# Scale and shift of the first head's input made together, two slices at a time, with no corrections afterwards

## The chip, the core and the metric

One core of a Trainium2 chip runs the whole kernel. The metric is device time in microseconds (us) of one execution. Its engines work in parallel and meet at semaphores: PE multiplies matrices, DVE, ACT and POOL work on vectors, SP starts transfers.

## The reference

One layer of a two-branch backbone over 128 context and 512 latent tokens, 2048 channels wide, in fp32. The part that matters here is the input side:

```
mod   = silu(c) @ w_ada + b_ada             # c_ctx for context tokens, c for latent tokens
shift, scale, gate = split(mod, 3)          # 2048 values each
h     = rms_norm(x, norm_w) * (1 + scale) + shift
proj  = h @ w_in                            # 9 parts of 8 heads x 128 columns
rq, rk, rv, rg, hq, hf_f, hf_b, hi, hg = split(proj, 9)
```

Retention (rq, rk, rv, gate rg) and a gated recurrence (hq, forget gates hf_f and hf_b, hi, gate hg) follow for each head, in both directions; then one output projection, a gated residual and a norm.

## The kernel before

**Layout.** `h` is kept transposed: 16 slices of 128 channels, each 128 x 640 tokens. Every fp32 factor of the large products is split into a high and a low part (`hT_hi`, `hT_lo`, `w_hi`, `w_lo`), and a product is three matmuls, high*high, low*high and high*low. The weights of a head come as 18 chunks of 512 KB (`load`, L477) into three raw slots; `split` has ACT write the high part (L664) and DVE the low part (L1167) into two slots. The work of all engines is written out by hand, chunk by chunk (`items(n, h, prev)`, `stage(n, h, prev)`), and meets at semaphores; the order is that of the code.

**Heads 1 to 7** project in this order: chunks 0 and 1 the queries hq (`chunk`, 320 token columns per matmul, two halves), chunks 2 to 9 the group hf_f, hf_b, rq, rk (`group_chunk`: 512 latent columns at a time, and the context tokens with the weights as the moving side), chunks 10 to 17 the token parts (`token_chunk`, L2103 to L2105).

**Head 0** is another matter, since `h` isn't there yet when it starts. `w_ada` arrives as 32 pieces of 1 MB (`load_ada`, L445; four slots), and PE multiplies them with silu(c) (`ada_chunk`, L1895), 32 rows of the array for each quarter of the channels. DVE copies the sum to a row (`modulation_row`, L1175), PE turns it into columns (`modulation_columns`, L1903 to L1906) and DVE adds bias and norm weight (`modulation`, L1201, L1207). In the kernel before, the first 16 pieces give **scale** only, four slices at a time. With it the slices are scaled and split (L675 on ACT, L1226 on DVE; L1214 and L1232 for the first four), and PE projects three of the five column parts with them (`ahead`, L1920), then the other two (`chunk`, L2036). The other 16 pieces give **shift** and are multiplied between those projections (`between_slices`). Since the five column parts were projected without shift, their missing term shift @ w_in is computed from five more loads of 1 MB of plain weights (`w_first`, L447): `correction` (L1984), a copy on DVE (L1284), `correction_transposes` (L1991), and biases in the copies of ACT (`corrected`, L718 to L725). For the token parts the shift is added to the slices themselves, two slices per token chunk: DVE (`shifted_input`, L1271), ACT (L681) and POOL (L1813).

**Queue of transfers.** SP issues head 0's loads in a fixed order, each `w_ada` piece when PE has used the piece four before it.

Of the kernel before, what the change touches and what calls it, by code (L numbers as in the profile page):

```python
# [34 lines left out]
P = 128  # L35
D_MODEL = 2048
# [5 lines left out]
HEADS = 8  # L42
# [25 lines left out]
AHEAD = 3  # L68
UNITS = 2 * AHEAD
X_LOADS = 4  # L70
SQUARES = 4
CORRECTIONS = 5
# [45 lines left out]
def layer(nc, x_prompt, x_sample, s_ret_f, s_ret_b, s_hg_f, s_hg_b, c, c_ctx,  # L118
          w_out, final_norm_w, x_columns, vectors, w_mod, w_first, w_gate, gate_bias, w_in, consts,
          y_prompt, y_sample, n_ret_f, n_ret_b, n_hg_f, n_hg_b):  # L120
    ctx = ExitStack()
    with ctx:
# [23 lines left out]
        SMALL = 448 + P + 4 * TILES + 3 * KT  # L146
# [79 lines left out]
        shift = var[:, 0:KT * QUAD].rearrange("p (k m) -> p k m", k=KT)  # L226
        shifting = (newt, rstd)
        x_total_ps = ps.rearrange("p b n -> p (b n)")[:, 4 * 512:4 * 512 + T]
        corr_row = o_two
# [14 lines left out]
        corr = sc(2 * CORRECTIONS).rearrange("p (i w) -> p i w", w=2)  # L244
# [36 lines left out]
        h_mod, h_hi, h_lo = Signal("h_mod"), Signal("h_hi"), Signal("h_lo")  # L281
        s_mod, s_hi, s_lo = Signal("s_mod"), Signal("s_hi"), Signal("s_lo")
        corr_rows, corr_out, corr_ready = Signal("corr_rows"), Signal("corr_out"), Signal("corr_ready")
        z_exp, r_fixed = Signal("z_exp"), Signal("r_fixed")
# [55 lines left out]
        def proj(i):  # L340

            return ps[:, 2 * (i % 2):2 * (i % 2) + 2, 0:HALF]

        def first_head(h):
            return isinstance(h, int) and h == 0

        def ahead_banks(i):

            return (2, A, 0)[i]

        def part(h, i):

            if first_head(h) and i < AHEAD:
                return ps[:, ahead_banks(i):ahead_banks(i) + 2, 0:HALF]
            return proj(i)
# [43 lines left out]
        def new_queries(h):  # L399

            return o_one if first_head(h) else hq_next[:, :]

        def grouped(h, n):

            return not first_head(h) and QUERY_CHUNKS <= n < COLUMN_CHUNKS
# [11 lines left out]
        def mods_known(piece):  # L417

            return 2 * (piece + 1) if piece <= QUARTERS else piece + 2 + QUARTERS
# [8 lines left out]

        def shifted_slices(n):

            return range(4) if n == 9 else range(2 * n - 16, 2 * n - 14) if 10 <= n < 16 else range(0)
# [8 lines left out]
        def _(sp):  # L440
            def load_ada(c):
                if c >= ADA_SLOTS:
                    sp.wait_ge(a_used.sem, a_used.at(c - ADA_SLOTS))
                if c < ADA_CHUNKS:
                    sp.dma_start(ada_raw[:, c % ADA_SLOTS, :], w_mod[c]).then_inc(a_landed[c % ADA_SLOTS].sem, 16)  # L445
                else:
                    sp.dma_start(ada_raw[:, c % ADA_SLOTS, :], w_first[c - ADA_CHUNKS]).then_inc(a_landed[c % ADA_SLOTS].sem, 16)  # L447
# [2057 lines left out]
```

## Time and profile before

| | us |
|---|---|
| median of 3 runs | 1438.04 (1437.69 to 1439.27) |
| the profiled execution | 1438.13 |
| its span in the trace | 1436.2 |
| PE busy | 1414.6 (98%) |
| DVE busy | 980.4 (68%) |
| ACT busy | 508.2 (35%) |
| POOL busy | 394.1 (27%) |

The profiled execution is 0.09 us above the median, and 1.9 us of it lie outside the span. In a window row, each engine's busy us stand with its instruction count in brackets, then PE's granted clock as a share of full speed, the mean busy share of the 16 transfer engines, and what they moved. In a timeline row, the first number is the start, the second the busy time of the merged instructions; a bracket gives idle time before and who ended it. PE matmuls overlap, so the pitch is the distance of starts. A plain fp32 matmul shows as two.

### The profile page before, as it was taken

The numbers are of one execution on the slowest core, as the hardware profiler recorded it, in microseconds if no ns is written. First come the engines' busy times: TensorE is split into PE (matmuls) and PEld (weight loads), VectorE is DVE, ScalarE is ACT, GpSimd is POOL, SyncE is SP. The second block draws the span as 40 slices with busy tenths as digits, with TensorE's granted clock in tenths as the row PEclk, the third lists the DMA queues.
The fourth block names the chain that finished last, engine by engine and source line by source line (L and its number), as shares of the span: only waits on it lengthen the run. The fifth ranks groups of instructions, "written<-read, shape, count | busy, mean of one in ns | idle before, by whom it ended". The sixth has DMA issues, their size and how long they took to land.

```text
span 1436.2 us, 26292 instructions
## 1 busy us (share of the span) xinstructions
PE 1414.6 (98%) x10558; PEld 1204.3 (84%) x10558; DVE 980.4 (68%) x1306; ACT 508.2 (35%) x912; POOL 394.1 (27%) x308
## 2 busy tenths in 40 slices
PE   7999999999999999999999999999999999999997
PEld 6998798889888988898889888988898888788886
DVE  5733996666878687878887888666566748632345
ACT  4322543333332433343334333433342334221234
POOL 0001563411342144214321532153115315301220
PEclk9999999999999999999999999999999999999999
DMA  9998322324333334333333333222223347183235
GB/s 379 378 363 356 92 90 74 96 67 141 114 134 94 127 126 126 101 125 124 119 99 121 126 118 110 67 81 89 96 67 96 87 149 255 46 279 117 88 103 205
DMA packets 69303, 201.93 MB, mean 141 GB/s; under 512 B 7872, under 2 KB 16336, under 8 KB 63440
## 3 DMA queue, kind: packets, MB, share of 16 engines
q1 hardware_dynamic: 69168, 200.39, 40.5%
q8 instruction: 83, 1.36, 0.4%
q14 instruction: 20, 0.16, 0.0%
q10 hardware_dynamic: 32, 0.02, 0.0%
HBM read 179.65 MB, written 16.53 MB: 137 GB/s over the span
## 4 chain that ended last, share of the span: by engine, by line
PE 93%; DMA 2%; DVE 2%; POOL 1%; ACT 1%; issue 1%; SPq 0%; DVEq 0%; ACTq 0%
PE ps L2103 10%; PE ps L2105 9%; PE ps L2104 9%; PE ps L2036 9%; PE ps L2056 7%; PE ps L2058 7%; PE ps L2057 7%; PE ps L2285 5%; PE ps L2287 5%; PE ps L2286 5%; PE ps L1920 3%; PE ps L2122 2%; PE ps L1895 2%; PE ps L2067 2%; PE ps L2065 2%; PE ps L2066 2%
## 5 line engine op out<-in xcount | busy, mean ns | idle before, releaser
L1167 DVE TENSOR_TENSOR w_lo<-area,w_hi 128x1024 fp32r<-128x1024 f32 x144 | 193.5, 1344 | 259.5 <-ACT w_hi L664 259.0
L664 ACT ACTIVATE w_hi<-area 128x1024 fp32r<-128x1024 f32 x144 | 152.4, 1058 | 469.4 <-PE ps L2105 243.9
L2103 PE MATMUL ps<-w_hi,hT_hi 128*128 128x512 f32 x640 | 253.5, 396 | 2.8 <-DVE w_lo L1167 2.8
L2105 PE MATMUL ps<-w_hi,hT_lo 128*128 128x512 f32 x640 | 249.6, 390 | 0.0
L2104 PE MATMUL ps<-w_lo,hT_hi 128*128 128x512 f32 x640 | 249.3, 390 | 0.0
L2056 PE MATMUL ps<-hT_hi,w_hi 128*128 128x512 f32 x448 | 178.0, 397 | 0.0
L2057 PE MATMUL ps<-hT_lo,w_hi 128*128 128x512 f32 x448 | 174.5, 390 | 0.0
L2058 PE MATMUL ps<-hT_hi,w_lo 128*128 128x512 f32 x448 | 174.5, 390 | 0.0
L2103 PEld LDWEIGHTS ps<-w_hi,hT_hi 128*128 128x128 f32 x640 | 120.2, 188 | 29.6 <-DVE w_lo L1167 3.9
L1790 POOL TENSOR_TENSOR area<-area 128x320 f32<-128x320 f32 x56 | 53.9, 963 | 326.3 <-PE ps L2122 273.7
L2105 PEld LDWEIGHTS ps<-w_hi,hT_lo 128*128 128x128 f32 x640 | 120.1, 188 | 25.4
L2104 PEld LDWEIGHTS ps<-w_lo,hT_hi 128*128 128x128 f32 x640 | 120.3, 188 | 23.6
L2285 PE MATMUL ps<-w_hi,hT_hi 128*128 128x512 f32 x296 | 116.9, 395 | 0.9 <-DVE w_lo L1632 0.9
L2287 PE MATMUL ps<-w_hi,hT_lo 128*128 128x512 f32 x296 | 115.4, 390 | 0.0
L2286 PE MATMUL ps<-w_lo,hT_hi 128*128 128x512 f32 x296 | 115.3, 390 | 0.0
L1632 DVE TENSOR_TENSOR w_lo<-area,w_hi 128x1024 fp32r<-128x1024 f32 x32 | 43.4, 1355 | 94.9 <-ACT w_hi L1010 94.8
L2058 PEld LDWEIGHTS ps<-hT_hi,w_lo 128*128 128x128 f32 x448 | 84.1, 188 | 17.8
L2056 PEld LDWEIGHTS ps<-hT_hi,w_hi 128*128 128x128 f32 x448 | 84.1, 188 | 17.5
L2057 PEld LDWEIGHTS ps<-hT_lo,w_hi 128*128 128x128 f32 x448 | 84.2, 188 | 16.4
L839 ACT ACTIVATE area<-area 128x1280 f32<-128x1280 f32 x56 | 71.2, 1275 | 70.9 <-DVE area L1435 66.3
L1421 DVE SCALAR_TENSOR_TENSOR gate_sums<-gate_raw,small,gate_sums 128x512 f32<-128x512 f32 x128 | 90.5, 767 | 0.0
L1801 POOL TENSOR_TENSOR area<-area 128x320 f32<-128x320 f32 x56 | 62.3, 1113 | 85.4 <-ACT area L839 85.4
(300 smaller groups left out, 2650.5 us busy)
## 6 DMA issues: line engine op xcount, KB each, us to landing
area<-in_w_in SPq DMA_DIRECT2D x144, 512.0 KB, 3.7
area<-in_w_mod SPq DMA_DIRECT2D x32, 1024.0 KB, 9.2
area<-in_w_out SPq DMA_DIRECT2D x38, 512.0 KB, 3.7
gate_raw<-in_w_gate SPq DMA_DIRECT2D x32, 512.0 KB, 3.7
area<-in_x_columns SPq DMA_DIRECT2D x4, 1280.0 KB, 9.7
area<-in_w_first SPq DMA_DIRECT2D x5, 1024.0 KB, 8.1
o_hi_scratch<-area SPq DMA_DIRECT2D x14, 320.0 KB, 2.2
o_lo_scratch<-area SPq DMA_DIRECT2D x14, 320.0 KB, 2.8
```

The costliest lines, as they stand in the source:

```text
L664: act.activation(w_hi[:, n % 2, :], raw[:, n % 3, :], ACT.Copy).then_inc(wt_hi.sem, 1)
L1167: v.tensor_tensor(w_lo[:, n % 2, :], raw[:, n % 3, :], w_hi[:, n % 2, :].bitcast(F32), ALU.subtract).then_inc(wt_lo.sem, 1)
L2036: ins = mm(out[s], wt[:, n % 2, w], x[:, k, s * HALF:(s + 1) * HALF], start=k == 0 and step == 0, stop=k == KT - 1 and step == 2)
L2056: mm(ps[:, bank, :], w_hi[:, n % 2, w], hT_hi[:, k, P:T], start=k == 0, stop=False)
L2057: mm(ps[:, bank, :], w_hi[:, n % 2, w], hT_lo[:, k, P:T], start=False, stop=False)
L2058: ins = mm(ps[:, bank, :], w_lo[:, n % 2, w], hT_hi[:, k, P:T], start=False, stop=k == KT - 1)
L2103: mm(out, hT_hi[:, k, tile_cols(t)], w_hi[:, n % 2, w], start=k == 0, stop=False)
L2104: mm(out, hT_hi[:, k, tile_cols(t)], w_lo[:, n % 2, w], start=False, stop=False)
L2105: i = mm(out, hT_lo[:, k, tile_cols(t)], w_hi[:, n % 2, w], start=False, stop=k == KT - 1)
L2285: mm(out, hT_hi[:, k, tile_cols(t)], hi, start=k == first, stop=False)
L2286: mm(out, hT_hi[:, k, tile_cols(t)], lo, start=False, stop=False)
L2287: return mm(out, hT_lo[:, k, tile_cols(t)], hi, start=False, stop=k == final)
```

## The change

Scale and shift come together. Piece order of `w_ada` is changed: a run of four pieces holds scale and shift of **two** slices (the first slice and the second slice have two pieces each). DVE normalizes a pair of slices ahead (`normed_input`), then multiplies and adds in one instruction (`modulated_input`), and the high and low parts hold the finished `h`. Head 0 then projects the same group as the other heads, slice by slice, all four parts (`first_group`), from chunks in the group's layout; the queries follow as chunks 8 and 9, in banks C and DD; the token parts need no shift any more. `correction`, `shifted_input`, `corrected`, `first_gates` and the five loads `w_first` are gone, and head 0 uses the group's copies, context transposes and reciprocals.

```diff
-            chunks = {6: 1, 9: 2, 11: 3, 13: 4, 15: 5, 17: 6, 20: 7, 24: 8, 28: 9, 32: 10, 36: 11}
-            for c_ in range(ADA_CHUNKS + CORRECTIONS):
+            chunks = {6: 1, 10: 2, 14: 3, 18: 4, 22: 5, 26: 6, 30: 7}
+            for c_ in range(ADA_CHUNKS):
                 load_ada(c_)
                 if c_ in chunks:
                     load(0, chunks[c_])
+            load(0, 8)
...
+            for e in range(WCHUNKS):                    # ACT
+                for k in range(WK * e, WK * (e + 1)):
+                    high_input(k)
+                if e < WCHUNKS - 1:
+                    split(0, e + 1)
...
+            def modulated_input(k):                     # DVE
+                dve.wait_ge(h_norm.sem, h_norm.at(k))
+                for w, tokens in CLASSES:
+                    x = x_in[:, k, tokens]
+                    i = v.tensor_scalar(x, x, mods[:, w, k:k + 1], shifts[:, w, k:k + 1], ALU.mult, ALU.add)
+                i.then_inc(h_mod.sem, 1)
...
+            for e in range(1, WCHUNKS):
+                split(0, e)
+                for k in range(WK * e, WK * (e + 1)):
+                    normed_input(k)
+                modulation_row(e + 1)
+                modulation(e + 1)
+                for k in range(WK * e, WK * (e + 1)):
+                    modulated_input(k)
+                for k in range(WK * e, WK * (e + 1)):
+                    low_input(k)
...
+            for e in range(1, WCHUNKS - 1):             # PE
+                c0 = (e + 1) * GROUP_CHUNKS
+                first_group(e, 0)
+                for c_ in range(c0, c0 + GROUP_CHUNKS):
+                    ada_chunk(c_)
+                first_group(e, 1, range(0, 1))
+                modulation_columns(e + 2)
+                first_group(e, 1, range(1, 5))
+            first_group(WCHUNKS - 1, 0)
+            first_group(WCHUNKS - 1, 1)
...
-            def correction(m):
-                for k in range(KT):
-                    rows = slice(k % 4 * QUAD, (k % 4 + 1) * QUAD)
-                    ins = mm(out[rows, :], shift[:, k, :], ada_raw[:, slot, tile_cols(k)], start=k < 4, stop=k >= KT - 4)
```

How PE's order moves, in the middle of the stage that makes the slices. Before (L1895 multiplies pieces of `w_ada`, 16 matmuls for one; L1920 are projections of one part; L1906 turns the row into columns):

```order
L1920 MATMUL ps<-hT_lo,w_hi 128x320 x2
L1920 MATMUL ps<-hT_hi,w_lo 128x320 x2
L1895 MATMUL ps<-area 32x128 x64
L1920 MATMUL ps<-hT_hi,w_hi 128x320 x2
L1920 MATMUL ps<-hT_lo,w_hi 128x320 x2
L1920 MATMUL ps<-hT_hi,w_lo 128x320 x2
L1906 MATMUL ps<-con,area 128x128
L1920 MATMUL ps<-hT_hi,w_hi 128x320 x2
```

After (L1744 to L1746 a part of the group, L1751 to L1753 the context tokens, L1728 the pieces, L1739 the columns):

```order
L1751 MATMUL ps<-w_hi,hT_hi 128x512
L1752 MATMUL ps<-w_lo,hT_hi 128x512
L1753 MATMUL ps<-w_hi,hT_lo 128x512
L1728 MATMUL ps<-area 32x128 x64
L1744 MATMUL ps<-hT_hi,w_hi 128x512
L1745 MATMUL ps<-hT_lo,w_hi 128x512
L1746 MATMUL ps<-hT_hi,w_lo 128x512
L1739 MATMUL ps<-con,area 128x128
L1744 MATMUL ps<-hT_hi,w_hi 128x512
```

A run of four pieces stood between projections worth 12 slice-parts of four slices before; after, between the 15 matmuls of the pair's first slice and the 15 of its second.

How DVE's order moves for the same stage. Before, one run of four slices (L1175 row, L1201 and L1207 columns, L1226 low parts, L1167 weights, L1220 and L1221 the normalizing of a later slice):

```order
L1175 COPY area<-ps 128x128
L1201 TENSOR_TENSOR small<-ps,small 128x4 x2
L1207 SCALAR_TENSOR_TENSOR small<-small 128x4 x2
L1226 SCALAR_TENSOR_TENSOR hT_lo<-area,small,hT_hi 128x128
L1226 SCALAR_TENSOR_TENSOR hT_lo<-area,small,hT_hi 128x512
...
L1167 TENSOR_TENSOR w_lo<-area,w_hi 128x1024
L1220 TENSOR_TENSOR area<-area 128x128
L1221 TENSOR_TENSOR area<-area 128x512
```

After, one pair (L1093 row, L1116 to L1119 scale and shift columns, L1132 multiply and add, L1137 low parts, L1085 the next weights):

```order
L1093 COPY area<-ps 128x128
L1116 TENSOR_TENSOR small<-ps,small 128x2x2
L1117 TENSOR_TENSOR small<-ps,small 128x2x2
L1119 SCALAR_TENSOR_TENSOR small<-small 128x2x2
L1132 TENSOR_SCALAR area<-area,small 128x128
L1132 TENSOR_SCALAR area<-area,small 128x512
L1132 TENSOR_SCALAR area<-area,small 128x128
L1132 TENSOR_SCALAR area<-area,small 128x512
L1137 TENSOR_TENSOR hT_lo<-area,hT_hi 128x640 x2
L1085 TENSOR_TENSOR w_lo<-area,w_hi 128x1024
```

Between the columns and the first low part stand four multiply-and-adds on DVE, and ACT's high part; before, ACT scaled and split in one instruction beside DVE.

At the end of the stage, on PE before, the last corrections stand ahead of the first token chunk:

```order
L2036 MATMUL ps<-hT_hi,w_lo 128x320 x2
L1984 MATMUL ps<-area 32x128 x48
L2103 MATMUL ps<-w_hi,hT_hi 128x512
L2104 MATMUL ps<-w_lo,hT_hi 128x512
L2105 MATMUL ps<-w_hi,hT_lo 128x512
```

After, the queries (L1839) stand right ahead of the first token chunk (L1889 to L1891):

```order
L1839 MATMUL ps<-hT_lo,w_hi 128x320 x2
L1839 MATMUL ps<-hT_hi,w_lo 128x320 x2
L1889 MATMUL ps<-w_hi,hT_hi 128x512
L1890 MATMUL ps<-w_lo,hT_hi 128x512
L1891 MATMUL ps<-w_hi,hT_lo 128x512
```

The five corrections and their transposes (L1991, inside the first token chunk) have gone, and nothing stands in their place there.

## Rows read from the trace of the kernel before

**Rows 1.** The page: the span, and each engine's busy us, share and instructions.

```profile
span 1436.2 us, 26292 instructions
PE 1414.6 (98%) x10558; PEld 1204.3 (84%) x10558; DVE 980.4 (68%) x1306; ACT 508.2 (35%) x912; POOL 394.1 (27%) x308
```

**Rows 2.** PE's waits: total us, times, longest us.

```profile
PE ps L2103 <- DVE w_lo L1167: 2.8, 2, 1.5
```

**Rows 3.** Windows of 10 us (columns as told above).

```profile
0.00:10.00 10.00, 5.21 (x26) 4.97 (x27) 1.61 (x8) 3.62 (x6) 0.20 (x4) 1.00 0.74 274
...
60.00:70.00 10.00, 10.00 (x172) 9.60 (x172) 6.40 (x14) 1.55 (x2) 0.00 (x0) 1.00 0.87 340
...
100.00:110.00 10.00, 10.00 (x171) 9.40 (x164) 4.83 (x22) 1.94 (x6) 0.00 (x0) 1.00 1.02 424
...
120.00:130.00 10.00, 10.00 (x144) 9.21 (x143) 2.70 (x7) 1.06 (x1) 0.00 (x0) 1.00 1.01 415
...
170.00:180.00 10.00, 8.74 (x39) 6.93 (x38) 9.61 (x12) 6.29 (x12) 6.34 (x3) 1.00 0.32 98
```

**Rows 4.** Loads from 0 to 142 us: count, size, median us from issue to landing.

```profile
area<-in_w_mod SPq DMA_DIRECT2D x32, 1024.0 KB, 9.2
area<-in_w_in SPq DMA_DIRECT2D x14, 512.0 KB, 8.7
area<-in_x_columns SPq DMA_DIRECT2D x4, 1280.0 KB, 9.7
```

**Rows 5.** PE's timeline: fillers, pieces of w_ada, projections of 320 columns.

```profile
27.65 2.50 PE L1929 MATMUL ps<-con 128*128 128x128 f32 x20
...
50.70 3.70 PE L1895 MATMUL ps<-area 128*32 128x128 f32 x128
54.33 0.56 PE L1920 MATMUL ps<-hT_hi,w_hi 128*128 128x320 f32 x2
...
55.71 0.45 PE L1920 MATMUL ps<-hT_lo,w_hi 128*128 128x320 f32 x2
56.00 0.46 PE L1920 MATMUL ps<-hT_hi,w_lo 128*128 128x320 f32 x2
...
65.19 3.70 PE L1895 MATMUL ps<-area 128*32 128x128 f32 x128
```

**Rows 6.** PE's timeline around and in the first token chunks.

```profile
136.66 1.08 PE L1984 MATMUL ps<-area 128*32 128x128 f32 x32 [0.68 <-DMA area<-in_w_first]
137.68 0.50 PE L2103 MATMUL ps<-w_hi,hT_hi 128*128 128x512 f32 x1
...
140.54 1.20 PE L1991 MATMUL ps<-con,area 128*128 128x32 f32 x10
141.58 0.48 PE L2103 MATMUL ps<-w_hi,hT_hi 128*128 128x512 f32 x1
...
150.51 0.39 PE L2103 MATMUL ps<-w_hi,hT_hi 128*128 128x512 f32 x1
...
158.44 0.39 PE L2105 MATMUL ps<-w_hi,hT_lo 128*128 128x512 f32 x1
```

**Rows 7.** Groups of DVE and ACT, 0 to 142 us: busy us, mean ns, idle before.

```profile
L1167 DVE TENSOR_TENSOR w_lo<-area,w_hi 128x1024 fp32r<-128x1024 f32 x12 | 14.7, 1223 | 15.8 <-ACT w_hi L664 15.6
L1221 DVE TENSOR_TENSOR area<-area 128x512 f32<-128x512 f32 x12 | 8.2, 684 | 0.0
L1232 DVE TENSOR_TENSOR hT_lo<-area,hT_hi 128x640 fp32r<-128x640 f32 x4 | 3.3, 822 | 0.1
L669 ACT ACTIVATE hT_hi<-area 128x640 fp32r<-128x640 f32 x4 | 2.9, 737 | 10.2 <-DVE area L1214 10.2
L1175 DVE COPY area<-ps 128x128 f32<-128x128 f32 x9 | 2.6, 291 | 24.3 <-PE ps L1895 20.3 <-issue 4.0
```

**Rows 8.** Groups over the whole span, for instructions the change adds to head 0.

```profile
L1550 DVE TENSOR_SCALAR area<-area,small 128x640 f32<-128x640 f32 x14 | 7.9, 607 | 0.0
L2075 PE MATMUL ps<-con,area 128*128 128x128 f32 x28 | 4.2, 272 | 0.0
```

More of the change, by code:

```diff
@@ L1906, in modulation_columns, with group_part @@
                     nc.tensor.transpose(ps[:, ada_bank(piece), 0:P], mod_row, ident).then_inc(row_tr.sem, 1)
-            def ahead(s, kks=range(ADA_K)):
-                n, quarter, i = s // 2, s // AHEAD, s % AHEAD
-                if kks[0] == 0 and s % 2 == 0:
-                    pe.wait_ge(wt_lo.sem, wt_lo.at(0, n + 1))
-                for kk in kks:
-                    k = quarter * ADA_K + kk
-                    w = slice((s % 2) * ADA_K * P + kk * P, (s % 2) * ADA_K * P + (kk + 1) * P)
-                    if i == 0:
-                        pe.wait_ge(h_lo.sem, h_lo.at(k))
-                    for step, (wt, x) in enumerate(((w_hi, hT_hi), (w_hi, hT_lo), (w_lo, hT_hi))):
-                        for half in range(2):
-                            ins = mm(ps[:, ahead_banks(i) + half, 0:HALF], wt[:, n % 2, w], x[:, k, half * HALF:(half + 1) * HALF],
-                                     start=k == 0 and step == 0, stop=k == KT - 1 and step == 2)
-                if kks[-1] == ADA_K - 1 and s % 2:
-                    ins.then_inc(wt_used.sem, 1)
+            def group_part(n, kk, i, k):
+                bank, w = GROUP_BANKS[i], slice(kk * WIDE + i * P, kk * WIDE + (i + 1) * P)
+                mm(ps[:, bank, :], w_hi[:, n % 2, w], hT_hi[:, k, P:T], start=k == 0, stop=False)
+                mm(ps[:, bank, :], w_hi[:, n % 2, w], hT_lo[:, k, P:T], start=False, stop=False)
+                return mm(ps[:, bank, :], w_lo[:, n % 2, w], hT_hi[:, k, P:T], start=False, stop=k == KT - 1)
@@ new lines, in group_context, with first_group @@
+            def group_context(n, kk, k):
+                w = slice(kk * WIDE, (kk + 1) * WIDE)
+                mm(ps[:, BB, :], hT_hi[:, k, 0:P], w_hi[:, n % 2, w], start=k == 0, stop=False)
+                mm(ps[:, BB, :], hT_hi[:, k, 0:P], w_lo[:, n % 2, w], start=False, stop=False)
+                return mm(ps[:, BB, :], hT_lo[:, k, 0:P], w_hi[:, n % 2, w], start=False, stop=k == KT - 1)
+            def first_group(e, kk, places=range(len(GROUP_PARTS) + 1)):
+                k = WK * e + kk
+                if kk == 0 and places[0] == 0:
+                    pe.wait_ge(wt_lo.sem, wt_lo.at(0, e + 1))
+                if places[0] == 0:
+                    pe.wait_ge(h_lo.sem, h_lo.at(k))
+                for i in places:
+                    if i < len(GROUP_PARTS):
+                        ins = group_part(e, kk, i, k)
+                        if k == KT - 1:
+                            ins.then_inc(pe_group.sem, 1)
+                    else:
+                        ins = group_context(e, kk, k)
+                        if kk == WK - 1:
+                            ins.then_inc(wt_used.sem, 1)
@@ L2048, in group_chunk @@
                 pe.wait_ge(wt_lo.sem, wt_lo.at(h, n + 1))
-                for i, bank in enumerate(GROUP_BANKS):
+                for i in range(len(GROUP_PARTS)):
                     if j == 0 and i == 0:
```

440 lines of the change are left out of this document (106 added, 334 removed).

## The prediction

> **What bounds the kernel now.** I read the page first. PE is busy 1414.6 of 1436.2 us, every other engine has slack [rows 1]. So time comes only from fewer or denser matmuls, or from PE's idle 21.6 us. The list of waits says where that is: behind the start-up, the largest is 2.8 us in two stalls of head 0's token chunks, waiting for the low weights of DVE [rows 2]. I then read the windows of head 0, the only head that the change rewrites. From 100 to 130 us PE is full and the transfers are full as well, 415 to 424 GB/s at a share above 1.0; from 60 to 70 us they reach 340, because SP must wait for slots that PE frees [rows 3]. So this stage has two limits close together, and the change moves both. From 140 us on transfers are idle and DVE is the busy one: 9.61 of 10 us between 170 and 180, where PE drops to 8.74 [rows 3]. Last I read PE's timeline: the first token chunk starts at 137.68 us, right behind the last correction, which had waited 0.68 us for its load [rows 6]. That instant is the mark against which I build the new stage.
>
> **Durations.** A 320-column matmul has a pitch of 0.147 us (two in 0.29) [rows 5]. A 512-column one has 0.2266 (35 from 150.51 to 158.44) [rows 6]. One slice through four parts is 24 of the first, 3.52 us, before, and 15 of the second, 3.40 us, after. Over 16 slices the change of form saves 1.9 us; the queries stay in the old form, 96 x 0.147 = 14.1. A run of four pieces of `w_ada` takes 3.63 (50.70 to 54.33). From run to run are 14.49 us, of which 72 matmuls take 10.56, so switching kinds and turning the row into columns cost 0.30 a run [rows 5].
>
> **PE through the new stage, step by step.** The fillers end at 30.15 [rows 5]. Piece 3 now stands ahead of them: 31.1. Two slices of the first pair (6.8), four pieces (3.8), 0.3 for columns and form changes, 0.3 for small waits: the second pair's run ends at 42.3.
>
> Then the first new wait. For pair 1 nothing lies between the run and the first slice that needs it. The chain is: row copy 0.29, columns, three small DVE operations, multiply-and-add, ACT's high part 0.74, low part 0.82 [rows 7]. The multiply-and-add is not in the trace in two pieces; as one over 640 columns with two per-partition scalars it takes 0.61 [rows 8], and that is my value. It can't be below it, and at worst is as slow as a two-tensor pass, 0.68 on 512 columns and some 0.2 for the short piece, 0.9 [rows 7]. The three small ones have no row of their form; each lies between nothing and the 0.29 of the row copy, and I take 0.5 for all with their waits (ends 0 and 0.9). Sum: 0.36 + 0.3 + 0.5 + 0.6 + 0.8 + 0.9, about 3.6. PE idles until 45.9; slice 3.4, run 3.8: the next run ends at 53.1.
>
> For pairs 2 to 6 the second slice of the pair before (3.40, plus 0.30) covers the chain. With the transposes placed behind the first part the chain is 0.3 longer, 3.95: PE stalls 0.25. PE's cycle is 3.63 + 6.80 + 0.30 + 0.25 = 11.0. The transfers' cycle is 4 x 1024 KB + 512 KB = 4.72 MB [rows 4], at 419 GB/s (mean of the two full windows) 11.25. Both are so near that the waits of the one at times add to the other: I take 11.3, five times 56.5, and 0.6 more for the first, since during the 3.6 us stall the four slots are full and SP can't issue. So the last run ends at 110.2. Transfers alone give a floor: by then 43.25 MB have to come (5.24 of x, 4.19 of weights, 33.55 of `w_ada`, 0.26 small), 2.74 in the first 10 us [rows 3], the rest at 419 GB/s: 106.7, and 0.95 for the last piece. Behind the run: the second slice with columns 3.7, stall 0.25, two slices 6.8: 120.95. Queries 14.1 and 0.1 for the switch: the token chunks start at **135.1, 2.6 us earlier**. The five corrections (L1984) with their wait and five loads of 1 MB are inside these 2.6 us, since 137.68 counted them.
>
> ACT evacuates the group and splits chunk 9 beside the queries, 7 us ahead of need. Chunk 8 is queued behind the last `w_ada` piece and lands some 10 us ahead of its use. The two con loads moved behind it are used only from the rotary step on. If one of these covers failed, PE would wait at the queries for 1.05 + 1.22, 2.3 us.
>
> **Token stage.** The five transposes of the corrections stand in the first token chunk: 140.54 to 141.58, 1.04 us gone [rows 6]. The two stalls of 2.8 us go [rows 2]: DVE loses 32 shift additions; it gains two context operations, a reciprocal, and four affine operations of 0.5 to 0.6 that ACT did, about 6 us against some 15 to 20. The new dependence is the context transposes, four fp32 ones on PE: 4 x 0.11 if pipelined, 4 x 0.27 if not [rows 8]; I take 0.45. They wait for ACT's context copy, made a whole query stage earlier. The retention scores wait for the rotated rk; its inputs are there at about 121 us, some 50 us ahead.
>
> **Sum.** 2.6 + 1.04 + 2.8 - 0.45 = 6.0 us less than the profiled execution's own 1438.13 (span 1436.2 [rows 1] and 1.9 outside it): 1432.1. That execution is 0.09 us above the median of the runs, so I forecast **1432.0 us**. Ends of the unknown prices: 0.3 to 0.6 more per pair for multiply-and-add and small operations, 5 pairs and the first, 3.6 us; the stalls half gone instead of gone, 1.4; the transposes 0.6; against it 0.25 x 5 + 1.5 if the two limits overlap perfectly. The forecast's own range is 1429.0 to 1435.1.
>
> **A rule against the change.** At 100 to 130 us the load stream reads 415 to 424 GB/s with DVE, ACT and PE at work [rows 3]. The Trainium skill (DMA: Bandwidth & Descriptors, Bandwidth, Where 436 GB/s comes from) says that for HBM-to-SBUF transfers the HBM side, about 358 GB/s per core, binds; its own table has 425 for one core on large transfers. By the 358 the 40.5 MB would take an estimated 113 us instead of 96.7, and this change would be a loss, some 1448. The trace disagrees with the 358, so I give that only a small chance.
>
> The granted clock stays 1.00 in the first 10 us, in which PE is busy for only 5.21 [rows 3]. The Trainium skill (TensorE: Matmul & The Clock Gate, What's actually happening) has idleness halve the clock. If the 3.6 us wait of pair 1 did so, the next slice would run at the lower level, 3.4 us more; the row at the start speaks against it.
>
> **Rivals.**
> *PE paces the stage.* Transfers run ahead, the chain fits under the slice. For it: 11.0 against 11.25 is thin, and the low parts of the first slice come early. Then five cycles at 10.8 and no 0.6: 3.1 us less, 1428.9. Against it: the floor of 106.7 lies only 3.5 us below my 110.2, so not much more can come.
>
> *The saving is eaten, no change to speak of.* The chain is a microsecond longer per pair (DVE's weight split and the normalizing, 1.22 + 1.6 us [rows 7], stand ahead of the row copy, and the weights of a pair land only one piece before its last). Each microsecond by which that group is late is paid by PE. Landing 3.5 us before the run's end, it is late by 0.4; at 1 us late, less 0.25 of slack to the transfers, 5 x 0.75 = 3.8: 1435.8. Against it: a slower PE lets the transfers get ahead, so the lateness limits itself.
>
> *Slower: the stage is bound by transfers below 419 GB/s.* Before, 4 MB came for 12 slice-parts of work in these cycles, 14.49 us [rows 5]; now for 8, so each per cent of rate costs 1 us of stage. The place is the wait of `ada_chunk` for its piece. From 10 us on 40.5 MB have to come, 96.7 us at 419 GB/s; it decides when that is 8.9 us longer (my 1432.0 to 1440.9, 0.2% above before), at 384 GB/s. At 340, the rate of the window 60 to 70 [rows 3], it would be 22.4 us longer: 1454.4. For it: that window. Against it: there the slots were empty by PE's order, and with the queue full no window is under 415.
>
> *The change doesn't do what it says*: corrections remain in some form. Excluded by the order on PE.
>
> **Chances.** Forecast 0.52, PE-paced 0.12, eaten 0.24, slower by transfers or by a chain too long 0.12. Measurement of this kernel can tell about 0.2%, 2.9 us, from no change: faster is under 1435.2, slower over 1440.9. The first two cases are faster, 0.64; the third is the same, 0.24; the last slower, 0.12. The range that should hold eight times in ten is 1428.5 to 1438.5.
>
> **What the profile after would show.** Right: waits of PE for low slices (hT_lo), one of about 3 us near 43 us and small ones after; waits for w_mod of 0 to 1 us per run; pitch 0.227 in the group; runs 11.3 us apart; transfers above 415 GB/s from 55 to 107 us; the first token chunk at about 135; no wait of head 0 for w_lo. Wrong: runs 12 us apart or more (then see whether hT_lo or w_mod ends the wait), a wait at the queries, the w_lo stalls still there, or a granted clock below 1.00 near 46 us.

## The result: slower by 0.3%, where 0.4% faster was forecast

| | before | after | forecast of after |
|---|---|---|---|
| median us (range, runs) | 1437.96 (1437.69 to 1439.27, 7) | 1442.84 (1441.77 to 1444.63, 7) | 1432.0 |
| profiled execution, us | 1438.13 | 1444.63 | 1432.1 |
| first token chunk of head 0 | 137.68 | 148.57 | 135.1 |
| first matmul of head 1 | 198.50 | 205.07 | 192.5 |

The ratio after to before is 1.0031, with a 95% interval of 1.0021 to 1.0041. The profiled execution of after is the slowest of its seven; the places below are read from it, so up to 1.8 us of its time are its own. The time lies outside the range of the forecast (1428.5 to 1438.5), in the case "slower", which had 0.12.

The loss is all ahead of head 1: its first matmul is 6.57 us late, the span 6.8 us longer. Inside head 0 the two halves have opposite signs. From the first token chunk to head 1, before took 60.8 us and after 56.5: 4.3 less, with 3.4 forecast. The stage that makes the slices ends 10.9 us later than before, where 2.6 earlier was forecast: the whole miss, 13.5 us, is there.

### The profile page after: what moved, and what is told of

Read it like the earlier page. It is cut to its first block, busy times and chain, and to the rows that moved or that the text cites. A ratio compares the mean times of both kernels' runs of the same rounds, so it can differ in the third digit from the quotient of the medians.

```text
span 1443.0 us, 25582 instructions
## 1 busy us (share of the span) xinstructions
PE 1412.7 (98%) x10247; PEld 1191.0 (83%) x10247; DVE 959.5 (66%) x1292; ACT 488.8 (34%) x877; POOL 360.2 (25%) x292
## 4 chain that ended last, share of the span: by engine, by line
PE 92%; DMA 5%; DVE 1%; SPq 1%; ACT 0%; issue 0%; POOL 0%; DVEq 0%; ACTq 0%
PE ps L1889 10%; PE ps L1891 10%; PE ps L1890 10%; PE ps L1744 8%; PE ps L1839 8%; PE ps L1746 8%; PE ps L1745 8%; DMA area<-in_w_mod 5%; PE ps L2069 5%; PE ps L2071 5%; PE ps L2070 5%; PE ps L1906 2%; PE ps L1753 2%; PE ps L1751 2%; PE ps L1752 2%; PE ps L1728 1%
## 5 line engine op out<-in xcount | busy, mean ns | idle before, releaser
L1085 DVE TENSOR_TENSOR w_lo<-area,w_hi 128x1024 fp32r<-128x1024 f32 x144 | 187.4, 1302 | 312.1 <-ACT w_hi L642 311.5
L1889 PE MATMUL ps<-w_hi,hT_hi 128*128 128x512 f32 x640 | 253.2, 396 | 0.0
L1891 PE MATMUL ps<-w_hi,hT_lo 128*128 128x512 f32 x640 | 249.5, 390 | 0.0
L1744 PE MATMUL ps<-hT_hi,w_hi 128*128 128x512 f32 x512 | 206.5, 403 | 4.8 <-DVE hT_lo L1137 4.8
L1746 PE MATMUL ps<-hT_hi,w_lo 128*128 128x512 f32 x512 | 200.9, 392 | 0.0
L1745 PE MATMUL ps<-hT_lo,w_hi 128*128 128x512 f32 x512 | 200.6, 392 | 0.0
L1889 PEld LDWEIGHTS ps<-w_hi,hT_hi 128*128 128x128 f32 x640 | 120.2, 188 | 25.6 <-issue 1.6
L1891 PEld LDWEIGHTS ps<-w_hi,hT_lo 128*128 128x128 f32 x640 | 120.1, 188 | 25.5
L1744 PEld LDWEIGHTS ps<-hT_hi,w_hi 128*128 128x128 f32 x512 | 97.0, 189 | 28.2 <-issue 8.5
L1746 PEld LDWEIGHTS ps<-hT_hi,w_lo 128*128 128x128 f32 x512 | 96.7, 189 | 21.0
L1745 PEld LDWEIGHTS ps<-hT_lo,w_hi 128*128 128x128 f32 x512 | 97.1, 190 | 18.5
L1472 DVE TENSOR_TENSOR w_lo<-area,w_hi 128x1024 fp32r<-128x1024 f32 x32 | 43.4, 1357 | 96.3 <-ACT w_hi L928 96.2
```

The lines of the kernel that those rows point to most:

```text
L1085: v.tensor_tensor(w_lo[:, n % 2, :], raw[:, n % 3, :], w_hi[:, n % 2, :].bitcast(F32), ALU.subtract).then_inc(wt_lo.sem, 1)
L1744: mm(ps[:, bank, :], w_hi[:, n % 2, w], hT_hi[:, k, P:T], start=k == 0, stop=False)
L1745: mm(ps[:, bank, :], w_hi[:, n % 2, w], hT_lo[:, k, P:T], start=False, stop=False)
L1746: return mm(ps[:, bank, :], w_lo[:, n % 2, w], hT_hi[:, k, P:T], start=False, stop=k == KT - 1)
L1889: mm(out, hT_hi[:, k, tile_cols(t)], w_hi[:, n % 2, w], start=k == 0, stop=False)
L1891: i = mm(out, hT_lo[:, k, tile_cols(t)], w_hi[:, n % 2, w], start=False, stop=k == KT - 1)
```

## The profile after

The page: PE is busy for 1.9 us less than before [rows 1], the span is 6.8 longer; PE waits more.

```profile
span 1443.0 us, 25582 instructions
PE 1412.7 (98%) x10247; PEld 1191.0 (83%) x10247; DVE 959.5 (66%) x1292; ACT 488.8 (34%) x877; POOL 360.2 (25%) x292
```

PE's waits. The stall of [rows 2] is gone; pieces of w_ada (L1728), low slices (L1744) and the row (L1739) hold it up now.

```profile
PE ps L1728 <- DMA area<-in_w_mod: 7.4, 5, 2.1
PE ps L1744 <- DVE hT_lo L1137: 4.8, 6, 3.1
PE ps L1739 <- DVE area L1093: 0.4, 1, 0.4
```

Windows, to lay beside [rows 3]. The granted clock is no longer 1.00 throughout, and the transfers have holes in the stage that was forecast as bound by them.

```profile
30.00:40.00 10.00, 10.00 (x111) 8.68 (x115) 3.06 (x9) 1.69 (x2) 0.00 (x0) 0.83 0.92 378
...
50.00:60.00 10.00, 9.75 (x148) 8.04 (x149) 3.96 (x8) 1.06 (x1) 0.00 (x0) 0.83 0.60 228
60.00:70.00 10.00, 9.34 (x125) 7.36 (x123) 3.62 (x10) 2.51 (x3) 0.00 (x0) 1.00 1.01 419
...
80.00:90.00 10.00, 9.56 (x153) 7.78 (x153) 6.51 (x15) 2.51 (x3) 0.00 (x0) 1.00 0.88 342
...
100.00:110.00 10.00, 9.54 (x154) 7.48 (x153) 4.89 (x11) 2.03 (x3) 0.00 (x0) 1.00 0.88 338
...
120.00:130.00 10.00, 8.53 (x59) 6.82 (x60) 7.45 (x16) 2.62 (x4) 0.00 (x0) 0.83 0.54 215
```

PE's timeline answers to [rows 5] and shows the start and pair 1. Piece 3, ahead of the fillers (L1776) by the change, is waited for 2.04 us. Then it takes 1.76 us where the same 32 matmuls took 1.08 three us earlier, and the fillers 3.42 where before they took 2.50. The first slice starts at 34.86. At pair 1, behind its wait of 3.08 us, two matmuls stand at the pitch of 0.3, and then seven at 0.43: 1.2 GHz instead of 2.4.

```profile
26.87 1.08 PE L1728 MATMUL ps<-area 128*32 128x128 f32 x32
...
30.00 1.76 PE L1728 MATMUL ps<-area 128*32 128x128 f32 x32 [2.04 <-DMA area<-in_w_mod]
31.68 3.42 PE L1776 MATMUL ps<-con 128*128 128x128 f32 x20
34.86 0.48 PE L1744 MATMUL ps<-hT_hi,w_hi 128*128 128x512 f32 x1
...
46.85 0.33 PE L1739 MATMUL ps<-con,area 128*128 128x128 f32 x1 [0.41 <-DVE area L1093]
50.25 0.47 PE L1744 MATMUL ps<-hT_hi,w_hi 128*128 128x512 f32 x1 [3.08 <-DVE hT_lo L1137]
50.56 0.48 PE L1745 MATMUL ps<-hT_lo,w_hi 128*128 128x512 f32 x1
50.84 0.63 PE L1746 MATMUL ps<-hT_hi,w_lo 128*128 128x512 f32 x1
51.26 0.63 PE L1744 MATMUL ps<-hT_hi,w_hi 128*128 128x512 f32 x1
...
53.82 0.54 PE L1744 MATMUL ps<-hT_hi,w_hi 128*128 128x512 f32 x1
54.20 0.39 PE L1745 MATMUL ps<-hT_lo,w_hi 128*128 128x512 f32 x1
...
55.45 3.70 PE L1728 MATMUL ps<-area 128*32 128x128 f32 x128
```

The chain of waits from 59 to 98 us (start, us, what) names what sets the later pairs. It closes on itself: a load of w_ada is issued when PE has used the fourth piece of a run; it lands 10.5 to 11.9 us later; it is itself the fourth piece of the next run; PE multiplies it, 1.1 us; the next load is issued. (From 97 to 109 us the chain runs over PE's slices instead; then it is back on a load, 12.1 us.)

```profile
59.87 11.34 DMA area<-in_w_mod
...
71.25 1.12 PE ps L1728 x32
...
72.39 10.51 DMA area<-in_w_mod
...
82.95 1.06 PE ps L1728 x29
...
84.09 11.89 DMA area<-in_w_mod
...
96.02 1.08 PE ps L1728 x32
```

And the hole at 80 us: SP issues nothing between 72.8 and 81.15, since all four slots are taken and PE multiplies slices. The transfers' share sinks with it.

```profile
81.15 2.08 SPq L425 DMA_DIRECT2D area<-in_w_mod  x3
```

```profile
56.00:80.00 24.00, 21.77 (x306) 17.33 (x298) 10.82 (x26) 3.96 (x5) 0.00 (x0) 1.00 0.94 380
80.00:84.00 4.00, 3.89 (x130) 3.42 (x129) 2.45 (x5) 1.06 (x1) 0.00 (x0) 1.00 0.70 231
```

So I had three suspects. **A, slots:** one run uses as many pieces as there are slots, so PE's use and the refill add up instead of overlapping. **B, chain:** the modulation on DVE and ACT (3.08 + 0.41 us at pair 1, 0.33 to 0.35 at five more) sets the cycle. **C, clock:** what costs is the low clock behind the waits.

## The experiments

Each was run beside the kernel before on the same chip. An interval reaches 1.2 to 2.3 us to each side, so two gains that differ by less than some 2 us can't be told apart by the medians. "Tokens" is the start of the first token chunk in the profiled execution (137.68 before, 148.57 after, 135.1 forecast).

| kernel | median us | before beside it | ratio, 95% interval | tokens |
|---|---|---|---|---|
| fifth slot | 1436.78 | 1438.55 | 0.9988 (0.9979 to 0.9997) | 140.87 |
| two and two | 1434.96 | 1438.55 | 0.9973 (0.9963 to 0.9984) | 139.64 |
| start in the old order | 1441.47 | 1438.55 | 1.0019 (1.0010 to 1.0029) | 145.80 |
| half loads | 1434.34 | 1438.55 | 0.9971 (0.9959 to 0.9983) | 139.13 |
| fillers in pair 1's wait | 1440.90 | 1438.97 | 1.0010 (1.0001 to 1.0018) | 145.34 |
| start + two and two | 1432.67 | 1438.97 | 0.9951 (0.9939 to 0.9964) | 137.69 |
| the same + fifth slot | 1432.68 | 1438.97 | 0.9952 (0.9939 to 0.9965) | 136.08 |
| start + fifth slot | 1435.40 | 1438.97 | 0.9972 (0.9962 to 0.9982) | 138.57 |
| kernel before + fifth slot | 1438.22 | 1439.24 | 0.9993 (0.9984 to 1.0002) | 136.88 |
| weights last | 1455.60 | 1439.24 | 1.0108 (1.0093 to 1.0124) | 160.12 |
| fillers first | 1440.78 | 1439.24 | 1.0009 (1.0000 to 1.0018) | 144.17 |
| three things mended | 1432.99 | 1439.15 | 0.9955 (0.9941 to 0.9968) | 137.75 |

### A fifth slot

```diff
-ADA_SLOTS = 4
+ADA_SLOTS = 5
+        def ada_slot(slot):
+            return ada_four[:, slot, :] if slot < 4 else gate_raw.rearrange("p s n -> p (s n)")
```

> One edit to the changed kernel: a fifth 1 MB slot for the pieces of w_ada, in space that is free until the gate's weights come. Theory A (slots and landing: a run uses four pieces in 3.6 us out of four slots, so the transfers stand still 2.3 to 2.5 us in every second cycle, and the last piece is released some 2 us behind its bytes): PE's waits for w_mod after the first pair (5.2 us in three pieces) go to under 1 us, runs 11.3 us apart instead of 12.7, and the time falls by 4 to 6 us, to 1437 to 1439. Theory B (chain: the modulation chain of DVE and ACT sets the pair's cycle): no change beyond 0.5 us, the waits for hT_lo grow by what those for w_mod lose. Theory C (clock: the lower granted clock behind each wait is what costs): at most 1 us, by the one low stretch behind run 7.

Against before it stands 6.6 us better than the changed kernel did (1.8 below it instead of 4.9 above). A had expected 4 to 6, so the gain is a little larger. Its window from 60 to 110 us: 413 GB/s, no hole. Its timeline around 80 us: a run without a wait for its fourth piece, and then 0.35 us for the low slice; six such waits stand 11.4 us apart.

```profile
60.00:110.00 50.00, 48.24 (x655) 38.95 (x654) 29.75 (x69) 11.49 (x14) 0.00 (x0) 1.00 1.01 413
```

```profile
77.94 2.83 PE L1732 MATMUL ps<-area 128*32 128x128 f32 x96
80.58 1.06 PE L1732 MATMUL ps<-gate_raw,area 128*32 128x128 f32 x32
81.57 0.50 PE L1748 MATMUL ps<-hT_hi,w_hi 128*128 128x512 f32 x1
...
85.73 0.47 PE L1748 MATMUL ps<-hT_hi,w_hi 128*128 128x512 f32 x1 [0.35 <-DVE hT_lo L1141]
```

The waits for hT_lo did not grow: the chain was not hidden behind the loads. A holds, B and C alone fall. Of the 7.7 us at the tokens, 6.5 lie in the five cycles and 0.9 behind them, where the changed kernel's profile has a low stretch and this one has none. With a slot more than a run uses the cycle is 11.4, near the forecast's 11.3; but PE no longer waits for a piece in it, so it is PE's own cycle, 11.05 and the 0.35 of waiting for the low slice, where the forecast had 10.7 and 0.25.

### Two pieces behind each slice

```diff
                 first_group(e, 0)
-                for c_ in range(c0, c0 + GROUP_CHUNKS):
-                    ada_chunk(c_)
+                ada_chunk(c0 + 2)
+                ada_chunk(c0 + 3)
                 first_group(e, 1, range(0, 1))
                 modulation_columns(e + 2)
                 first_group(e, 1, range(1, 5))
+                if e < WCHUNKS - 2:
+                    ada_chunk(c0 + 4)
+                    ada_chunk(c0 + 5)
```

> One edit to the changed kernel: a pair's four pieces stand two behind the first slice and two behind the second slice of the pair before, instead of all four in one run; at pair 1 two of them fill part of the wait for the chain. Theory A (slots and landing): slots come back twice a cycle, the transfers do not stand still; waits for w_mod fall below 1.5 us in all and the time falls by 5 to 7 us. Theory B (chain): the chain gets 1.9 us more cover at pair 1 and the rest of the waits for hT_lo stay; 1.5 to 3 us less. Theory C (clock): with pieces in pair 1's wait the first slice of pair 1 runs at full clock: 1.6 us less beside the cover, about 3 in all, and no more.

8.5 us better against before than the changed kernel (3.6 below instead of 4.9 above), a little more than A expected, with four slots and no more memory. The waits on the line of the pieces (first row) and for low slices (second) up to the tokens:

```profile
PE ps L1728 <- DMA area<-in_w_mod: 3.5, 4, 2.3
PE ps L1744 <- DVE hT_lo L1137: 1.8, 2, 1.5
```

2.3 of the first row are piece 3 at the start. The chain has shorter waits too, 1.8 instead of 4.8 us, since now two pieces stand between a row's last piece and the slice that needs it. The profiles part the 8.9 us at the tokens: 4.1 are shorter waits for pieces behind the start, 3.4 shorter waits of the chain, 3.1 the low stretches at 50 and 122 us, which this profile doesn't have, and against them stands 1.7 of a longer low stretch at the start. So only about half of the gain is A's; the fifth slot shows A by itself.

### Half of each load

```diff
-                sp.dma_start(ada_raw[:, c % ADA_SLOTS, :], w_mod[c])
+                sp.dma_start(ada_raw[:, c % ADA_SLOTS, 0:D_MODEL // 2], w_mod[c][:, 0:D_MODEL // 2])
```

> The changed kernel with each piece of w_ada loaded by half (512 KB of 1 MB), the loaded half multiplied twice, so PE's work is the same and the modulation is computed from other numbers. It takes the transfers out of the stage. Theory A (transfers and slots): waits for w_mod vanish after the first pair, runs 11.0 to 11.3 us apart, piece 3 is there in time: 8 to 11 us less, about 1433. Theory B (chain): waits for hT_lo take their place at 1 us or more per pair: 3 to 5 us less (the start alone). Theory C (clock): the clock stays low behind pair 1's wait, which is still there: of the 1.6 us nothing comes back.

The second half of each piece is never loaded, so this kernel's outputs are not the layer's. 9.1 us better against before than the changed kernel, 9.4 at the tokens. The window of 60 to 70 us moved 222 GB/s. The chain's waits are those of the fifth slot to the digit (first row), and one wait for a piece is left (second row):

```profile
PE ps L1744 <- DVE hT_lo L1137: 5.2, 7, 3.1
PE ps L1728 <- DMA area<-in_w_mod: 1.7, 1, 1.7
```

So even with half the bytes a wait of this kind can occur, at 78.8 us. The chain has its load there:

```profile
66.72 12.05 DMA area<-in_w_mod
```

This load of 512 KB took as long to land as the full ones in the changed kernel, while 222 to 244 GB/s were moved in the windows from 60 to 80 us. Why is open, and with it whether the landing of 10.5 to 12.1 us is bytes over rate alone. That the missing slot makes PE pay for the landing is shown either way. Theory C's condition held: the clock was low behind pair 1's wait in this run as well.

### The start

```diff
-            ada_chunk(3)
             idle(10)
             first_group(0, 0, range(0, 2))
-            modulation_columns(1)
-            first_group(0, 0, range(2, 5))
+            ada_chunk(3)
+            first_group(0, 0, range(2, 3))
+            modulation_columns(1)
+            first_group(0, 0, range(3, 5))
```

> One edit to the changed kernel: the ten filler matmuls and the first two parts of the first slice stand ahead of piece 3 again, as in the kernel before, so PE does not wait 2.04 us for that piece and keeps its clock. If the start's 3.8 us (first slice at 34.9 instead of 31.1) is PE's order there, then run 1 ends 2.5 to 3.5 us earlier, and, if the stage behind it is paced by PE or by the chain (B), the time falls by the same 2.5 to 3.5 us. If the stage behind it is paced by the transfers (A), most of it is given back in longer waits for w_mod: 0.5 to 2 us less.

```diff
-            ada_chunk(3)
             idle(10)
+            ada_chunk(3)
```

> One edit to the changed kernel: only the ten filler matmuls are put ahead of piece 3 again; the parts of the first slice stay behind it. The forecast had counted piece 3 in front of them at nothing but its own 0.95 us. If the wait of 2.04 us for that piece and the low clock behind it (piece 3 1.76 instead of 1.08 us, fillers 3.42 instead of 2.50) are the whole miss there, the first slice starts at 31.6 instead of 34.86 and run 1 and the queries come 2.5 to 3.2 us earlier; the clock stays 1.00 from 30 to 40 us. Time 1440 to 1441.5. If the clock falls there for another reason, it is 0.83 still and 1 to 1.6 us of that stay.

Old order: pair 1's run ended 2.8 us earlier, the tokens came 2.8 earlier; nothing was given back in longer waits for w_mod (5.2 us, as in the changed kernel), against what A had expected. Two differences of the clock about cancel in this: behind pair 1's wait it stayed low longer (the slice took 6.33 us instead of 5.20), and behind the last run it did not fall. Slots explain that as well, once seen as a loop: PE's use of a piece issues the next load, so the loop as a whole shifts with PE. The medians give 2.0 us against before, the spans 2.5. Fillers first: PE's timeline at its start is the one that I had forecast, piece 3 and first slice without a wait and at full clock.

```profile
27.61 2.50 PE L1776 MATMUL ps<-con 128*128 128x128 f32 x20
30.16 1.08 PE L1728 MATMUL ps<-area 128*32 128x128 f32 x32
31.17 0.50 PE L1744 MATMUL ps<-hT_hi,w_hi 128*128 128x512 f32 x1
```

Pair 1's run ended at 42.7 (forecast 42.3, changed kernel 46.4), 3.7 us earlier where 2.5 to 3.2 were expected. The tokens came 4.4 us earlier: these 3.7 and 1.6 because the clock stayed full behind pair 1's wait, less 0.9 of longer waits for w_mod (6.0 instead of 5.2). The median stands 1.5 above before instead of 4.9. Of the 3.7 us of the start, 2.0 are the wait and 1.6 the low clock behind it (0.68 in the piece, 0.92 in the fillers).

### Fillers in pair 1's wait

```diff
             modulation_columns(2)
+            idle(12, A)
             for e in range(1, WCHUNKS - 1):
```

> One edit to the changed kernel: twelve filler matmuls in PE's wait of 3.1 us for the first slice of pair 1, into a bank that is empty then. PE still waits as long for the chain. Theory C (clock): that slice keeps the full clock, its pitch 0.227 us instead of 0.425, and everything behind it comes 1.6 us earlier; since a run gives the slots back where PE stands, the transfers restart earlier too and nothing is given back: 1.4 to 1.8 us less. If the low clock is not from the wait (a theory that it follows the work done, not the pause): pitch 0.425 stays, no change. If the transfers alone pace the stage: R2 is 1.6 us earlier, the queries 0 to 0.5.

```profile
48.16 2.84 PE L1776 MATMUL ps<-con 128*128 128x128 f32 x24
51.40 0.47 PE L1744 MATMUL ps<-hT_hi,w_hi 128*128 128x512 f32 x1 [0.40 <-DVE hT_lo L1137]
...
54.98 1.29 PE L1728 MATMUL ps<-area 128*32 128x128 f32 x39
```

The slice starts as late against its row (3.40 us behind L1739, as in the changed kernel) and takes 3.58 instead of 5.20: C's 1.62 us, exactly there. The median gained 2.9 us against before, more than expected; in this execution no low stretch stood behind the last run, and the waits for w_mod past pair 1 came to 3.7 us instead of 5.2. Why these fell I can't say from one profile. Against them, the low stretch at its start was longer: the first slice stood at 35.98, not 34.86.

### Start and pieces together, with and without the slot

> The two edits together: pieces two and two behind the slices, and fillers with two parts of the first slice ahead of piece 3. Measured apart they brought 7.9 us and 1.4 us (run medians) or 8.5 and 2.5 (spans). Slots theory: with two and two the transfers are full from 60 to 110 us (417 to 419 GB/s), so an earlier start of PE meets a transfer limit: 0.5 to 1.5 us beyond two and two, about 1434. Coupling theory (a delay of PE is passed on in full, as in the run with the start alone: run 1 2.80 us and the queries 2.76 us earlier): the full 2.5, about 1432.5.

> Pieces two and two, the start in the old order, and a fifth slot. If, with two and two, the transfers at 417 to 419 GB/s are what is left as a limit, a fifth slot brings only what it holds in advance at the start (up to 1 us), since the total of bytes is the same: 1432 to 1433.5. If slots are still what limits, 2 us or more beyond the run without the fifth slot. If PE and the chain pace it by now, nothing.

> Fifth slot and the start in the old order, the run of four pieces as in the changed kernel. With five slots the pairs were 11.40 us apart, PE never waiting for w_mod and 0.35 us per pair for hT_lo. So the 2.8 us of the start should pass in full to the queries (124.0 instead of 126.80), unless the transfers, full at 404 to 424 GB/s from 60 to 110 us, now end a wait: then 1 to 2 us. Time 1434 to 1435.5; the wait of 3.08 us at pair 1 and the low clock behind it stay.

Start and two-and-two: 6.3 us below before, 2.7 beyond two-and-two alone: the coupled theory, the full 2.5. This is the fastest order that needs no more memory than before: 0.9951. The fifth slot adds nothing to it in the medians (1432.68), although from 60 to 110 us PE then never waits and 417 GB/s flow. Its tokens came 1.6 us earlier in the profile, and the profiles don't say why: each has one low stretch that costs 1.6 to 1.7 us, that with four slots from 20 to 24 us, that with five from 48.3 to 51.7 us. Start with the fifth slot but one run of four: 3.6 below; tokens 2.3 earlier than with the slot alone, 2.8 expected.

### The kernel before with a fifth slot

> The kernel before with the same fifth 1 MB slot for w_ada. The question: is a fifth slot a gain of its own, or does it only mend what the change broke? Slots theory: the kernel before spreads its pieces, at most four together behind 12 slice-parts, and PE waits only 0.68 us for a load in that stage; so the slot brings nothing beyond 0.7 us, 1437.8 to 1438.9. If four slots are too few for any order, its window of 340 GB/s (60 to 70 us) fills and it gains 2 us or more.

0.9993, with 1 in the interval: no gain that could be told. Its window of 60 to 70 us went from 340 to 374 GB/s and the tokens came 0.8 us earlier, the wait of 0.68 [rows 6] and little else. Four slots are too few for the changed order, not for this kernel.

### Weights last

```diff
-            chunks = {6: 1, 10: 2, 14: 3, 18: 4, 22: 5, 26: 6, 30: 7}
+            chunks = {7: 1, 11: 2, 15: 3, 19: 4, 23: 5, 27: 6, 31: 7}
```

> One edit to the changed kernel: in the queue of transfers each pair's 512 KB of weights stand behind the pair's fourth piece instead of ahead of it. If the last piece's landing is what PE waits for at the run, that piece comes 1.2 us earlier (512 KB at 419 GB/s) and the waits for w_mod (1.57, 1.49, 2.11 in the changed kernel) lose up to 1.2 each: 1 to 3.5 us less in all. Against it, the weights come up to 2.4 us later than before relative to their use, and their split stands ahead of the row copy on DVE: chain theory has the waits for hT_lo grow from 0.35 to 1 or more per pair, which eats the gain or more. If the missing slots alone set the cycle (transfers can't start), only the order of landing changes and the time stays within 1 us.

1.0108, 16.4 us above before, 11.5 worse than the changed kernel: far more than any theory said. DVE's timeline (idle time before in brackets) shows the split of the weights held up, and behind it, in the order of the code, the row copy on which PE then waits:

```profile
74.12 1.23 DVE L1085 TENSOR_TENSOR w_lo<-area,w_hi 128x1024 fp32r<-128x1024 f32 x1 [8.54 <-ACT w_hi L642]
75.26 0.28 DVE L1124 TENSOR_TENSOR area<-area 128x128 f32<-128x128 f32 x1
...
76.86 0.28 DVE L1093 COPY area<-ps 128x128 f32<-128x128 f32 x1
```

```profile
77.21 0.35 PE L1739 MATMUL ps<-con,area 128*128 128x128 f32 x1 [3.41 <-DVE area L1093]
...
78.21 0.63 PE L1746 MATMUL ps<-hT_hi,w_lo 128*128 128x512 f32 x1
```

The waits for w_mod shrank as theory A had it (0.40, 0.57, 0.31 instead of 1.57, 1.49, 2.11). In every second cycle it paid 3.4 us for the row and a low clock behind it. The landing of the weights was on the edge of the path all along, as the rival "eaten" had it; in the changed kernel it just fitted: in the cycle at 84 us the row copy starts at 84.30, straight behind the normalizing, 0.3 us after the run's last piece.

### Three things mended

Fillers first, fifth slot and fillers in pair 1's wait together, all other work in the order forecast.

> The changed kernel with the three things mended that the runs so far point to, and nothing else: fillers ahead of piece 3, a fifth slot, twelve fillers in pair 1's wait. The order of all real work is the one forecast. If these three causes are the whole miss (apart: 4.4, 7.7 and 1.6 us at the first query matmul, in part the same microseconds), the first token chunk starts at 135.5 to 137.0 us (forecast 135.1, in the changed kernel 148.57), pairs 11.4 us apart, and the time is 1431.5 to 1433.5, the forecast being 1432.0. If something else took part of the miss, the first token chunk stands at 138 us or later and the time is over 1434.5.

1432.99, inside the expected 1431.5 to 1433.5, where the forecast was 1432.0, and against its own kernel before 6.2 us less, where 6.0 were forecast. The tokens stand at 137.75, just outside the expected 135.5 to 137.0; the sums of squares in the start-up ran at the low clock in this execution, 1.6 us that the forecast's source did not have:

```profile
20.02 1.87 PE L1790 MATMUL ps<-con 128*128 128x512 f32 x2 [1.75 <-ACT con L636]
```

In the changed kernel's profile that row reads 1.12. Its other four executions lie between 1432.38 and 1433.18; this one was the slowest, 1434.32.

## Why the prediction was wrong

**The step that failed is the sum of the new stage.** It had piece 3 at its own 0.95 us and nothing for its landing, took the larger of two cycles where they add up, and had nothing for the low clock. Forecast against the profile after (the end of a run is, as in the forecast, where the matmul behind it starts or could have started):

| | forecast | after | miss |
|---|---|---|---|
| pair 1's run ends | 42.3 | 46.37 | 4.1 |
| from there to the end of pair 2's run | 10.8 | 12.71 | 1.9 |
| from there to the end of the last run | 57.1 | 63.4 | 6.3 |
| from there to the tokens | 24.9 | 26.1 | 1.2 |
| token stage against before | -3.4 | -4.3 | -0.9 |
| sum, of unrounded terms | | | 12.5 (1444.6 against 1432.1) |

Two of the signs that the prediction had named for being wrong came: runs 12 us apart or more, ended by w_mod, and a low clock behind pair 1's wait.

- **"Piece 3 now stands ahead of them: 31.1."** I counted the moved piece at its own 0.95 us, and not when it lands. The median of [rows 4], 9.2 us, would not have helped: this load is issued at 6.55 and lands 23.40 us later, at 29.95, behind the loads of x and the pieces ordered before it. In the kernel before, the fillers and one part stood ahead of it, PE came to it at 31.24, and nothing showed. Shown by the two start runs: 2.0 us of wait and 1.6 of clock, most of the 4.1.
- **PE's cycle 11.0, the transfers' 11.25, "I take 11.3".** The sizes were near (PE's 0.4 short, by the fifth slot's 11.4), the rule to combine them was wrong. With as many slots as pieces in a run, the fourth piece of a run can only be ordered when the fourth of the last one is used. The cycle is then landing (10.5 to 12.1 us in the chain, about the 11.25 for 4.72 MB) plus 1.1 of use: an estimate of 12.4. Measured were 63.4 us in five cycles, a mean of 12.7; singly they took 13.2, 11.7, 13.1, 11.8 and 13.7, so PE is clearly late at every second run, and at the others about when the piece lands (82.90, PE at 82.95). Five slots gave 11.4. I had written "during the 3.6 us stall the four slots are full and SP can't issue", at 0.6 us and for pair 1 only; the same is true of every 7 us in which PE multiplies slices. The sentence "with the queue full no window is under 415" rested on the windows that were shown. The order of the kernel before did not keep the queue full either: besides the 340 of [rows 3], 50 to 60 us have 351, 80 to 90 have 345, and 90 to 100 the lowest of the stage,

```profile
90.00:100.00 10.00, 10.00 (x125) 9.42 (x128) 1.23 (x1) 2.24 (x3) 0.00 (x0) 1.00 0.74 282
```

  PE had enough other work there to wait for none of it; behind the change it has not.
- **The clock.** "The row at the start speaks against it" was the wrong inference. Rows of after show the granted clock at half behind three waits (30, 50 and 122 us), which cost 1.6, 1.6 and 1.5 us. The Trainium skill (TensorE: Matmul & The Clock Gate, What's actually happening) has idleness halve the clock; the trace agrees at these three, and of the 3.4 us that I priced for a whole slice at the low level 1.6 came. I had let a row of start-up, where PE's work had gaps and the clock stayed, overrule it, and gave it no chance at all.
- **The chain was nearly right**: 3.6 us forecast at pair 1 from the run to the slice (its terms add up to 3.46), 3.8 measured (46.4 to 50.25), in which PE idles for 0.41 + 3.08; 0.25 a pair, 0.33 to 0.35 measured. The multiply-and-add took 0.34 + 0.54 = 0.8 us with overlap, nearer its upper end (0.9) than my 0.61; small operations 0.16 each; the low parts 0.82.
- **The token stage was right and better**: both w_lo stalls gone, transposes gone, 4.3 us.
- **The rivals.** "Slower: the stage is bound by transfers below 419 GB/s" named the right wait (the pieces) with the wrong cause. The rate did not sink while loads of 1 MB were queued: 419 GB/s from 60 to 80 us, 407 from 84 to 104. The Trainium skill's 358 GB/s (DMA: Bandwidth & Descriptors, Where 436 GB/s comes from), a limit per core that is half of what two cores share, bound nothing here either. That rival also counted every us of later transfers in full, though by the prediction's own floor the first 2.5 us of them were free (107.65 against 110.2). What was missing among the rivals was the count of slots against the count of pieces in a run.
- **The range.** Its upper end, 1435.1, does not follow from the terms named for it: 3.6, 1.4 and 0.6 us above 1432.0 are 1437.6 together. The result lies beyond that too.

That the start, the slots and the clock are the causes and not companions is shown by the mended run: with them gone, the same order of work gives the forecast gain of 6 us. They aren't additive: singly they brought 3.3, 6.6 and 2.9 us against before, 12.8 in sum, together 11.0. That the sum also comes within 1 us of the forecast has some luck in it: the tokens start 2.7 us later than forecast there (1.6 of it the low clock at 20 us), and the token stage behind them took 56.5 us as in the changed kernel, 0.9 less than forecast.

## What to carry to other kernels

Before adding PE's cycle and the transfers' cycle as a maximum, count the buffers against the pieces used in one burst: if they are equal, use and refill follow one another and the cycle is their sum. Breaking the burst in two was worth 8.5 us here, about half of it by shorter waits for loads, and cost no memory; a fifth buffer was worth 6.6, and nothing that could be told in the kernel before. A load that moves earlier on PE has to be priced by when it lands, and a new wait of 2 to 3 us on PE by half speed behind it too; cheap filler matmuls take that part away.

## What the runs showed of the hardware

- **The clock falls behind some waits and not others.** In or behind pair 1's wait of 3.08 us the granted clock went to half, at the latest 2 us behind its end, in six profiled executions (the changed kernel, fifth slot, start in the old order, half loads, start with fifth slot, weights last), and stayed 1.00 in one (fillers first). With the waits of 2.04 to 2.51 us for piece 3 it fell in all five, and with the three of 3.4 us for the row in weights last each time. With the ten waits of 1.3 to 2.3 us for w_mod in the changed kernel, the two start runs and half loads it fell in two (2.11 and 2.25 us), and not in others of 1.89 and 2.06. With the 1.75 us at 20 us, which every kernel has, it fell in two of fourteen. Short waits are not safe: in the kernel with start, two-and-two and fifth slot it fell at 48.3 us, behind waits of 1.13 and 0.87 us with one piece between them. Most low stretches cost 1.5 to 1.7 us; some lasted about twice as long and cost 2.6 to 2.8 (for instance at the start of two-and-two and of the kernel with fillers in pair 1's wait, and behind pair 1's wait in the old order). This is also much of what differs between executions of one kernel, as far as the profiles, one for each kernel, can say. The window of the fillers-first kernel around its 3.08 us wait, clock 1.00:

```profile
46.00:51.00 5.00, 4.42 (x47) 3.56 (x51) 1.17 (x2) 1.21 (x2) 0.00 (x0) 1.00 0.88 360
```

- **A queue that has run dry costs more than the issue.** In the hole at 80 us the first of three loads was issued at 81.15, and traffic was back to 400 GB/s only past 83 us; the chain has the last load in front of the hole land at 82.90, though the full traffic had ended near 80.5. The fixed part shows by itself in two loads of 8 KB that SP issues at the start of the kernel before, 1.6 and 2.2 us from issue to landing:

```profile
small<-in_c_ctx SPq DMA_DIRECT2D x1, 8.0 KB, 1.6
small<-in_c SPq DMA_DIRECT2D x1, 8.0 KB, 2.2
```

  The Trainium skill (DMA: Bandwidth & Descriptors, Anatomy of one DMA) gives, for transfers that GpSimd issues, some 2 us fixed each, most of it the write's confirmation; the trace agrees with the size for SP's loads (what it is made of no run shows). While other loads of 1 MB were queued the rate was 407 to 419 GB/s all the same, so there it was hidden.
